# Decoder layer on one Trainium2 core: rows of experts 30 and 31 kept as a tile of their own and scattered last

## What is computed

```python
g_idx = argmax(x @ w_group + b_group)                  # one of 4 groups
top_v, top_i = top_k(logits of the 8 experts of that group, 2)
expert = g_idx * 8 + top_i                             # 2 experts of 32
h = silu(xb @ w_e_gate[e]) * (xb @ w_e_up[e])          # D_EXPERT = 512
y += weight * (h @ w_e_down[e])
x = layer_norm(2 ** 0.25 * x + y, ln2_g, ln2_b)
```

## Time and profile before

| | us |
|---|---|
| median of 3 runs (lowest, highest) | 1254.37 (1253.46, 1254.44) |
| the profiled execution's own time | 1253.62 |
| its span in the trace | 1251.6 |
| TensorE busy | 1226.5 (98%) |
| VectorE, ScalarE busy | 674.8, 427.9 |
| expert part, from the first gate product to the end | 782 to 1251.6 |

### The profile page before, as it was taken

How to read it: one execution, slowest core, us unless ns; L and a number is a source line. 1 busy time by engine, 2 the same in 40 slices (tenths; PEclk the granted TensorE clock), 3 DMA queues, 4 the chain that set the end, 5 groups by cost and what they waited for, 6 DMA issues and landing times.

```text
span 1251.6 us, 16410 instructions
## 1 busy us (share of the span) xinstructions
PE 1226.5 (98%) x6166; PEld 824.6 (66%) x6166; DVE 674.8 (54%) x1066; ACT 427.9 (34%) x619; POOL 60.6 (5%) x67
## 2 busy tenths in 40 slices
PE   9999999999999999999999999999999999999887
PEld 8888888888888888888888886333343334333333
...
GB/s 244 103 98 91 102 64 89 107 169 91 93 68 101 84 67 101 84 84 84 84 68 101 171 395 421 393 412 410 417 413 414 409 414 416 416 407 415 411 424 210
DMA packets 144574, 286.10 MB, mean 229 GB/s; under 512 B 11909, under 2 KB 109301, under 8 KB 120960
## 3 DMA queue, kind: packets, MB, share of 16 engines
...
...
## 4 chain that ended last, share of the span: by engine, by line
PE 86%; DMA 9%; DVE 3%; ACT 1%; issue 1%; SPq 0%; DVEq 0%; ACTq 0%; POOL 0%; POOLq 0%
PE bank L1582 18%; PE bank L1584 18%; PE bank L1583 18%; PE bank L1925 15%; DMA m_raw<-in_w_e_up_dram 9%; PE bank L1957 7%; PE bank L1981 4%; PE bank L1909 1%; DVE wo_lo L929 1%; PE bank L1667 1%; PE bank L1950 1%; PE bank L1737 1%; PE bank L1658 0%; PE bank L1660 0%; PE bank L1659 0%
## 5 line engine op out<-in xcount | busy, mean ns | idle before, releaser
L929 DVE TENSOR_TENSOR w_lo<-raw,w_hi 128x1024 fp32r<-128x1024 f32 x120 | 148.3, 1239 | 181.5 <-ACT w_hi L586 180.3
L1925 PE MATMUL bank<-m_raw,xe 128*64 128x512 f32 x984 | 233.3, 598 | 10.5 <-DMA m_raw<-in_w_e_up_dram 8.9
L1582 PE MATMUL bank<-xt_hi,w_hi 128*128 128x512 f32 (+1 forms) x584 | 226.7, 388 | 0.3 <-DVE xt_lo L929 0.3
L1584 PE MATMUL bank<-xt_hi,w_lo 128*128 128x512 f32 (+1 forms) x584 | 225.6, 386 | 0.0
L1583 PE MATMUL bank<-xt_lo,w_hi 128*128 128x512 f32 (+1 forms) x584 | 225.5, 386 | 0.0
L925 DVE TENSOR_TENSOR x<-x,bank 128x1024 f32<-128x1024 f32 x120 | 141.1, 1218 | 99.5 <-PE bank L1981 98.5
L586 ACT ACTIVATE w_hi<-raw 128x1024 fp32r<-128x1024 f32 x120 | 126.3, 1058 | 160.4 <-PE bank L1584 157.8
L1925 PEld LDWEIGHTS bank<-m_raw,xe 128*64 128x64 f32 x984 | 70.6, 136 | 132.3 <-issue 130.7
L1582 PEld LDWEIGHTS bank<-xt_hi,w_hi 128*128 128x128 f32 x584 | 109.7, 188 | 23.5 <-issue 1.9
L1584 PEld LDWEIGHTS bank<-xt_hi,w_lo 128*128 128x128 f32 x584 | 109.7, 188 | 22.4
L1583 PEld LDWEIGHTS bank<-xt_lo,w_hi 128*128 128x128 f32 x584 | 109.7, 188 | 21.7
...
## 6 DMA issues: line engine op xcount, KB each, us to landing
m_raw<-in_w_e_gate_dram SPq DMA_DIRECT2D x64, 1024.0 KB, 26.1
m_raw<-in_w_e_down_dram SPq DMA_DIRECT2D x61, 1024.0 KB, 26.3
m_raw<-in_w_e_up_dram SPq DMA_DIRECT2D x59, 1024.0 KB, 25.5
raw<-in_w_in_dram SPq DMA_DIRECT2D x88, 512.0 KB, 3.8
raw<-in_w_ret_o_dram SPq DMA_DIRECT2D x16, 512.0 KB, 3.4
...
m_split<-in_w_e_up_dram SPq DMA_DIRECT2D x10, 512.0 KB
raw<-in_w_out_dram SPq DMA_DIRECT2D x8, 512.0 KB, 3.8
```

The source lines that it names most:

```text
L929: return dve.tensor_tensor(dst, a, b_r.bitcast(F32), ALU.subtract)
L1582: pe.matmul(dst, sh, mh, start=first and x == 0, stop=False)
L1584: ins = pe.matmul(dst, sl, mh, start=False, stop=last and x == n - 1)
L1925: last = pe.matmul(bank[side:side + ROWS, 0, :], xe[:, 4 * half + k, :], weights(w, FE * k, FE), start=half == 0 and k == 0, stop=half == ...
```

## The change

**Rows.** The 64 first rows of expert 30 and the 64 first rows of expert 31 form a fifth tile of 128 rows, `late_rows`, whose token numbers are in `late_t` and `late_idx`. It starts at zero. For experts 24 to 29 TensorE makes, beside the four tiles, a fifth product with a small one-hot `late_pick` (128 x 128: which of the expert's rows belong to which of the late rows) in banks 2 and 3, and VectorE adds it to `late_rows` (`add_late`). Because banks 2 and 3 hold tile 2 before that, the product waits for `z_added` to count tile 2. The residual of these rows, ALPHA times the gathered rows, is kept in `base` by ScalarE. At the end TensorE sums `late_rows`, expert 30 and expert 31 in `z_late`.

**Normalization.** The four tiles of 128 tokens are normalized from `x2` as it is after expert 29, tile 0 in front of silu of expert 31, tile 1 to 3 behind it. For tiles 0 and 1 the product with the inverse deviation is on ScalarE (`scale_rows`), the addition of `ln2_b` on POOL. They are stored by SP. The fifth tile is normalized last, and POOL scatters its 128 rows over the stored ones by an indirect DMA, once all four stores are complete.

**Constants.** `ln2_g` and `ln2_b` come as four short rows, and TensorE and ScalarE spread them over the partitions at the ends of iterations 23 to 27 (`make_constant`), together with the row of late token numbers `t_row`. The two loads of 512 KB behind the last weights are gone.

**Ring.** From unit 152 (gate and up of expert 26 have units 154 to 157) the ring has 20 slots; slots 20 and 21 hold the new tiles.

The core of the diff:

```diff
+SHRINK, FEWER = 152, 20
+SHARED = (GROUPS - 1) * PER_GROUP
+CONSTS = SHARED - 1
+assert SHRINK % MRING == FEWER and LAST - 1 > SHARED
+def slot_of(n):
+    return n % MRING if n < SHRINK else (n - SHRINK) % FEWER
+def fill_of(n):
+    return n // MRING + 1 if n < SHRINK else SHRINK // MRING + 2 + (n - SHRINK) // FEWER
...
-                    sp.wait_ge(m_done, n + 1 - MRING)
-                if n % MRING == MRING - 1:
+                    sp.wait_ge(m_done, n + 1 - (MRING if n < SHRINK else FEWER))
...
+                if e == NEAR:
+                    sp.wait_ge(xe_turned, 1)
+                    for k, v in enumerate((io["ln2_g"], io["ln2_b"])):
+                        sp.dma_start(ln2_rows[ROWS + 2 * k:ROWS + 2 * k + 2, :], v.rearrange("a (k n) -> (a k) n", k=2)).then_inc(ln2_in, 16)
             load_down(LAST)
-            sp.wait_ge(m_done, M_END - MRING + 4)
-            sp.dma_start(ln2[:, 0, :], row(io["ln2_g"])).then_inc(ln2_in, 16)
-            sp.dma_start(ln2[:, 1, :], row(io["ln2_b"])).then_inc(ln2_in, 16)
+            for t in range(TT):
+                if t < 2:
+                    sp.wait_ge(pads_ok, t + 4)
+                else:
+                    sp.wait_ge(f_late, 2 * t - 2)
+                sp.dma_start(out_view[t], ln_out[:, t, :]).then_inc(stored, 16)
             sp.wait_ge(ovf_ready, 1)
...
+                if e == LAST:
+                    pool.wait_ge(base_ok, 1)
                 gather_rows(first_x[0:ROWS, e:e + 1])
+            for t in range(2):
+                pool.wait_ge(f_ok, t + 1)
+                pool.tensor_tensor(ln_out[:, t, :], ln_out[:, t, :], ln2[:, 1, :], ALU.add).then_inc(pads_ok, 1)
+            pool.wait_ge(stored, 16 * TT)
+            pool.wait_ge(f_late, 6)
+            pool.indirect_dma_start(out[0], bass.IndirectOffsetOnAxis(ap=late_idx[:, 0:1], axis=0), late_out[:, :], None,
+                                    bounds_check=last_x, oob_is_err=False).then_inc(scattered, 16)
...
+                if e + 2 >= LAST - 1:
+                    half = ROWS * (e + 3 - LAST)
+                    act.activation(base[half:half + ROWS, :], xg[0:ROWS, :], ACT.Copy, scale=ALPHA).then_inc(base_ok, 1)
...
+                if CONSTS <= e < CONSTS + 5:
+                    act.wait_ge(consts_made, e - CONSTS + 1)
+                    k = e - CONSTS - 1
+                    dst = t_row[:, :] if k < 0 else ln2[:, k // 2, 512 * (k % 2):512 * (k % 2) + 512]
+                    copy(dst, bank[:, 4, 0:dst.shape[1]]).then_inc(consts_out, 1)
...
+            def scale_rows(t):
+                act.wait_ge(f_inv, 3 * t + 3)
+                act.activation(ln_out[:, t, :], ln_out[:, t, :], ACT.Copy, scale=stats[:, 12 * t + 4:12 * t + 5]).then_inc(f_ok, 1)
...
+            tile_moments(0)
             gate_rows(gu_unit(LAST), LAST)
+            act.wait_ge(eps_set, 1)
+            row_std(0)
             ht_out(LAST, ht_last)
-            rows_high(2)
+            tile_moments(1)
+            row_std(1)
+            scale_rows(0)
             y_high(down_unit(LAST - 1), 1, y_hi, first_w[:, LAST - 1:LAST])
-            rows_high(3)
+            tile_moments(2)
+            row_std(2)
+            scale_rows(1)
             y_high(down_unit(LAST), 4, y_hi_last, first_w[:, LAST:LAST + 1])
+            tile_moments(3)
+            row_std(3)
+            act.wait_ge(late_made, LAST - SHARED)
+            row_mean(TT, z_late, TT + 1)
+            row_squares(TT, TT + 1)
+            row_std(TT)
...
+            for half, e in ((0, LAST - 1), (ROWS, LAST)):
+                step(dve.tensor_copy(late_t[half:half + ROWS, :], first_t[half:half + ROWS, e:e + 1]))
+                step(dve.tensor_copy(late_idx[half:half + ROWS, :], first_t[half:half + ROWS, e:e + 1]))
...
+            def build_late_pick(dst, e):
+                dve.tensor_scalar(dst[:, :], t_row[:, :], first_t[:, e:e + 1], None, ALU.is_equal).then_inc(late_pick_ok, 1)
+            def add_late(e):
+                n = e - SHARED
+                dve.wait_ge(late_made, n + 1)
+                dve.wait_ge(late_added, n)
+                z = late_rows[:, :].rearrange("p (b n) -> p b n", b=2)
+                tt(z, z, bank[:, 2:4, :], ALU.add).then_inc(late_added, 1)
...
-            for e in range(LAST):
+            for e in range(LAST - 1):
                 if e:
                     add_z(4 * (e - 1), e == 1, (0, 1))
-                if e == LAST - 1:
-                    dve.wait_ge(m_done, gu_unit(LAST - 1) + 2)
-                    step(dve.tensor_copy(ident_r[:, :], ident[:, :]))
-                    step.wait()
-                    rows_low(0)
-                    rows_low(1)
                 gate_up_rows(e + 1)
                 if e:
                     add_z(4 * (e - 1), e == 1, (2, 3))
                 build_pick(pick, first_t[:, e:e + 1])
-                if e == LAST - 1:
-                    rows_low(2)
+                if e == SHARED:
+                    dve.wait_ge(consts_out, 1)
+                    step(dve.memset(late_rows[:, :], 0.0))
+                    step.wait()
+                if e > SHARED:
+                    add_late(e - 1)
+                if e >= SHARED:
+                    build_late_pick(late_pick, e)
                 y_low(e, 1, y_lo, y_hi, first_w[:, e:e + 1])
-            dve.wait_ge(h_turned, LAST + 1)
-            build_pick(pick_last, first_t[:, LAST:LAST + 1])
-            rows_low(3)
+            a = 4 * (LAST - 2)
+            dve.wait_ge(base_ok, 2)
+            dve.wait_ge(late_added, LAST - 2 - SHARED)
+            step(tt(late_rows[:, :], late_rows[:, :], base[:, :], ALU.add))
+            dve.memset(mv[:, 0:1], EPS).then_inc(eps_set, 1)
+            dve.wait_ge(consts_out, 5)
+            step.wait()
+            add_z(a, False, (0, 1))
+            centre(ln_out[:, 0, :], rows_of(0), 0, 1)
+            gate_up_rows(LAST)
+            add_z(a, False, (2, 3))
+            inverse(0, 1)
+            add_late(LAST - 2)
+            build_late_pick(late_pick, LAST - 1)
+            build_late_pick(late_pick_last, LAST)
+            centre(ln_out[:, 1, :], rows_of(1), 1, 2)
+            inverse(1, 2)
+            y_low(LAST - 1, 1, y_lo, y_hi, first_w[:, LAST - 1:LAST])
+            centre(ln_out[:, 2, :], rows_of(2), 2, 3)
+            inverse(2, 3)
+            scaled(ln_out[:, 2, :], 2, 3)
             y_low(LAST, 4, y_lo_last, y_hi_last, first_w[:, LAST:LAST + 1])
-            dve.memset(mv[:, 0:1], EPS).then_inc(eps_set, 1)
+            centre(ln_out[:, 3, :], rows_of(3), 3, 4)
+            inverse(3, 4)
+            scaled(ln_out[:, 3, :], 3, 4)
+            centre(late_out, z_late, TT, TT + 1)
+            inverse(TT, TT + 1)
+            scaled(late_out, TT, TT + 1)
...
+            def late_sums(pair, choose, high, low, first):
+                for y in (high, low):
+                    for b in range(2):
+                        side = ROWS * b
+                        last = pe.matmul(pair[:, b, :], choose[side:side + ROWS, :], y[side:side + ROWS, :], start=first and y is high, stop=y is low)
...
+                if e > SHARED:
+                    pe.wait_ge(z_added, 4 * (e - 1) + 3)
+                    pe.wait_ge(late_pick_ok, e - SHARED)
+                    late_sums(bank[:, 2:4, :], late_pick, y_hi, y_lo, True).then_inc(late_made, 1)
                 if e + 2 < EXPERTS:
+                    if CONSTS < e <= CONSTS + 5:
+                        pe.wait_ge(consts_out, e - CONSTS)
                     turn_x(e + 2)
                 down(e, ht, 1, (0,))
                 if e == LAST - 1:
...
             pe.wait_ge(z_added, 4 * (LAST - 1))
+            pe.wait_ge(late_added, LAST - 1 - SHARED)
+            for b in range(2):
+                pe.matmul(z_late[:, b, :], ident[:, :], late_rows[:, 512 * b:512 * b + 512], start=True, stop=False)
             pe.wait_ge(ylo_ok, LAST)
-            pe.wait_ge(pick_ok, LAST + 1)
-            for t in range(TT):
-                if t == 2:
-                    pe.wait_ge(h_ok, LAST + 1)
-                if t == 3:
-                    pe.wait_ge(ht_ok, LAST + 1)
-                rows_so_far(t)
```

230 lines of the change are left out of this document (131 added, 99 removed).

## The result

The changed kernel takes **1268.56 us** (median of 4 runs, 1267.45 to 1270.06) against 1254.40 (1253.46 to 1255.10, 4 runs) for the kernel before beside it: ratio 1.0114, 95% interval 1.0097 to 1.0132. It is slower by 14 us, where 6 were forecast. Its profiled execution took 1268.73, with a span of 1266.9.

What follows compares the result with a forecast made beforehand. Weights set the pace with TensorE 1.6 us quicker per expert, then an engine chain. Span 1234.9 + 18.7 + 0.05 + 3.55 + 0.4 = 1257.6 against 1251.6, +6.0 us, giving a time of 1260.4; range 1254.5 to 1264.7.

Steps and rivals of the forecast that it cites:

- What bounds the kernel: Weights set the pace at 15.47 us per expert, TensorE having 1.6 us to spare; a chain of engines follows the last wait.
- H: Moment when expert 31's rows are transposed and ScalarE's copy starts: 1228.40 before, forecast 6.5 us later at 1234.9.
- Part 1, the stall: Iterations 25 to 30: TensorE's fifth product waits for VectorE's tile 2, 1.67 + 0.56 us; own pace becomes 16.08 us.
- Part 2, the constants: Ends of iterations 25 to 27: three 128x512 float32 products on TensorE at 0.45 us each, 1.35 us (0.7 to 2.7).
- The start: Second half of gate and up of expert 26 was taken to start at 1144.01, as in the earlier trace.
- The ring of 20 slots: Weight ring, costed at nothing; the rival that it binds gave 1260.4 to 1265 us, chance 0.04.
- Part 3, up to the last data: From H to the last normalized data: 18.7 us, VectorE setting the end, with POOL's addition and VectorE's pass overlapping.
- H + 17.1: Low end of the tail: last data 17.1 us behind H if ScalarE's list sets the end instead of VectorE.
- Part 3, the scatter: End of the kernel: POOL's scatter of the late rows, 2.6 + 0.94 = 3.55 us, unhidden, then 0.4 to the end.
- The waits did not swallow the product: Rival: DMA waits absorb TensorE's 2.2 us per iteration, expert 31 starts on time; not slower, 1253.5 us, chance 0.20.
- The scatter's rival: Rival at the end: the scatter costs 6.5 us like a loaded gather instead of 3.55; 1263.4 us, chance 0.09.

Runs made afterwards that it cites:

- e1_move: Changed kernel with the fifth product of iterations 25 to 30 moved behind the first half of `down`; 1256.59 us, ratio 1.0021 to the kernel before.
- e8_warm_all: Changed kernel with six unused 128x128 products on TensorE ahead of the fifth product's wait in each of iterations 25 to 30; 1264.17 us.
- e2_const_dma: Changed kernel with `ln2_g` and `ln2_b` loaded by two broadcast loads behind the last weights, without TensorE's four products and ScalarE's copies of them; 1272.86 us.

## Why the prediction was wrong

The direction and the place were right; the time is 3.9 us above the top of the range.

**What bounds the kernel (right).** Weights were the pace, with 1.6 us to spare: with the stall taken off the path by e1_move, waits for DMAs came back and H is 1229.80.

**Part 1, the stall (right in its mechanism and size, one consequence missing).** 1.67 us of idleness were worked out, 1.55 to 1.57 measured, and the iteration takes 16.20 us for 16.08. What failed is a term that had no place in the sum: it let a stall cost only its own length. `down` behind it was priced at 3.65 and 1.94 us as in the earlier trace rows, from a trace whose two longest waits in that stretch, 1.50 and 1.51 us, had left the clock at 1.00. With the stall the granted clock fell to 0.5 twice, and 3.3 us were added. e8_warm_all gives them back.

**Part 2, the constants (mis-sized).** Taken at 0.45, bounds 0.22 and 0.9; measured 1.05, above the upper bound. The step that failed is the reading of the row: x16 in the earlier trace rows counts records, and a float32 product leaves two of them. `gate_up_half` issues 8 products of 64 output partitions, so one of those is 0.45, and a product over all 128, as the constant is, is two of them. The row thus said 0.9, and the bounds should have begun there. With 1.05 the term is 3.15 instead of 1.35. e2_const_dma shows it: 3.3 us earlier without them.

**The start (not in the forecast).** I set gate and up of expert 26 at 1144.01 in both kernels. Over the kernels run here that start lies between 1143.6 and 1146.65, whatever the edit, so the 1.2 us lie within the spread of the weights' arrival; whether a part of them is a cost of the change is not shown, since the kernel before was traced once. The constants have no part in it: e2_const_dma starts at 1145.12 without them. The ring of 20 slots shows no cost: in the stretches shown between the last wait and the last weight the DMA's share is 0.98 to 1.03. That TensorE's lateness would not be caught up was right.

**Part 3, up to the last data (18.7 forecast, 19.0 measured, for partly other reasons).** That POOL and VectorE slow each other was right, and POOL's additions took 2.35. The price was put on the wrong side: POOL stayed under the 2.7 us for which it was priced alone, and VectorE paid, 2.0 us in a second pass and 0.5 in a first. In the earlier trace rows VectorE had started first (682.09 against 682.62) and POOL paid, 2.15 for 1.36; here POOL had started first (1250.56 against 1250.68). The traces fit an order in which the later one pays, but no run turned it round. And the first pass was priced at 1.42, the row of the second pass in the earlier trace rows. The first pass of the kernel before takes 1.41 too, but it reads PSUM; from SBUF with its stride it is 2.1 to 2.2. (The terms of "H + 17.1" add up to 17.0; only the low end of the range hangs on it.) Against that, ScalarE's list ran quicker, with `y_hi_last` at H + 8.2 for 9.0, and POOL was out of the way earlier. ScalarE's last deviation, forecast for H + 15.4, came at H + 16.4, since its mean of the late tile waited 2.17 us for `y_lo_last`, a chain that I had not followed. The errors nearly cancel; that the sum came out is luck.

**Part 3, the scatter (mis-sized, with one error hidden in it).** 3.55 + 0.4 and 0.05 forecast, 5.7 measured. The landing took 3.2 for 2.6, as the estimate by the Trainium skill had it ("DMA: Bandwidth & Descriptors", Anatomy of one DMA). But the earlier trace rows count from the start of the issue to the landing, so the 0.94 for POOL's issue was added to a time that holds an issue already: 3.55 against 3.2 is 0.35 too much. What is missing lies on both sides: 0.85 us pass on POOL between the last data and its issue, for which 0.05 was taken, and 1.65 between the landing and the end, for which 0.4 was read from a kernel whose last store SP had issued. The upper bound of 6.5 held it.

**The rivals.** The waits did not swallow the product, since 1.55 + 0.56 was more than what was to spare. The scatter's rival put 6.95 us behind the last data, nearer to the 5.7 than the forecast's 4.0, but not for its reason: the landing took 3.2 and not 6.5, and alone it gave 1263.4. The range failed because it held only the terms that I had: the low clock was none, and the constants' bound was too low.
